# The stores of the attention rows, begun by ScalarE on its own DMA queue instead of by SyncE

## The reference

```python
proj = einsum('btd,de->bte', x, w_in) + b_in          # q, k, v, conv value, conv gate
q, k = rope(q, pos), rope(k, pos)
attn = banded_window_attention(q, k, v, sinks)        # 8 heads of 64, 2 kv heads, window 128
u    = ca * sigmoid(cg)
conv = silu(layer_norm(depthwise_causal_conv(u)))     # width 31, 512 channels
mix  = concat([attn, conv]) @ w_out + b_out
h    = layer_norm(ALPHA * x + mix)
f    = hier_moe(h)                                    # top-1 group of 4, top-2 of its 8 experts
y    = layer_norm(ALPHA * h + f)
```

## Time and profile before

| | before |
|---|---|
| median of 3 runs | 1359.54 us |
| profiled execution, its own time | 1357.34 us |
| span of its trace | 1355.5 us |
| busy: PE, DVE, ACT, POOL | 1251.7, 737.0, 537.2, 471.5 us |
| busy shares | 92%, 54%, 40%, 35% |
| mean granted TensorE clock | 0.971 |
| DMA queue of SP (q1): share of the 16 engines' span | 47.2% |
| DMA queue of ACT (q10) | 0.8% |

### The profile page before, as it was taken

The page is one execution under the profiler, slowest core; times in us unless marked ns, Lnnn a source line. Parts: engine busy times, 40 slices in busy tenths (PEclk is TensorE's granted clock), DMA queues, the critical chain, the costliest instruction groups (busy, mean ns, idle before and its releaser), DMA issues.

```text
span 1355.5 us, 21260 instructions
## 1 busy us (share of the span) xinstructions
PE 1251.7 (92%) x5579; PEld 600.6 (44%) x5580; DVE 737.0 (54%) x2093; ACT 537.2 (40%) x883; POOL 471.5 (35%) x633
## 2 busy tenths in 40 slices
PE   8999998999999998799999999899999999999910
PEld 3444445666666665345555545333333333333300
DVE  2434334565465555468888887544444444444348
ACT  0000001344344433423333332366666656666544
POOL 5113210000000000345555554355666666665321
PEclk9999999999999998899999999999999999999965
DMA  6375645231221174256666544289899999999686
GB/s 260 95 220 161 182 150 164 79 112 60 78 71 48 63 234 147 98 201 219 220 220 190 153 143 140 76 260 336 273 325 366 328 290 344 318 367 354 192 273 261
DMA packets 91256, 273.41 MB, mean 202 GB/s; under 512 B 14888, under 2 KB 41088, under 8 KB 78038
## 3 DMA queue, kind: packets, MB, share of 16 engines
q1 hardware_dynamic: 73975, 226.53, 47.2%
q0 software_dynamic: 14384, 42.32, 13.0%
q10 hardware_dynamic: 2807, 3.53, 0.8%
HBM read 212.80 MB, written 66.40 MB: 206 GB/s over the span
## 4 chain that ended last, share of the span: by engine, by line
PE 46%; issue 30%; DVE 11%; DVEq 6%; DMA 3%; ACT 2%; POOL 1%; POOLq 1%; ACTq 1%; SPq 1%
PE P L1130 13%; PE bank_S L1152 9%; PE M L1130 6%; PE bank_S L744 4%; PE P L744 3%; DVEq L1723 3%; PE bank_T L744 2%; PE M L744 2%; DVE route L1728 2%; PE M L1138 1%; DVE work L1685 1%; PE bank_S L918 1%; DMA work<-conv_rows 1%; DMA big<-sum_rows 1%; ACT work L1447 1%
## 5 line engine op out<-in xcount | busy, mean ns | idle before, releaser
L1397 ACT ACTIVATE big<-big 128x2048 f32 x76 | 145.0, 1910 | 121.1 <-issue 71.8
L1130 PE MATMUL P<-big,work 128*64 x416 | 188.0, 595 | 1.7 <-DVE work L1943 1.5
L1131 PE MATMUL P<-big,work 128*64 128x512 f32 x416 | 188.0, 595 | 0.0
L783 PE MATMUL P<-big,work 128*128 128x256 f32 (+1 forms) x512 | 172.6, 493 | 3.7 <-DMA work<-in_xt_prompt 3.7
L2134 POOL DMA_INDIRECT work<-h_rows,piece_idx x148 | 141.9, 959 | 63.2 <-issue 40.4
L1152 PE MATMUL bank_S<-big,work 128*64 x304 | 136.7, 592 | 1.0 <-DVE work L1927 1.0
L1154 PE MATMUL bank_S<-big,work 128*64 128x512 f32 x304 | 136.7, 592 | 0.0
L2050 POOL TENSOR_SCALAR work<-work 128x1 f32<-128x1 f32 (+1 forms) x17 | 3.8, 221 | 364.4 <-DVE work L1606 364.3
L783 PEld LDWEIGHTS P<-big,work 128*128 128x128 f32 x512 | 96.0, 191 | 74.3 <-issue 64.3
L918 PE MATMUL P<-big,work 128*128 128x512 f32 x256 | 115.9, 606 | 6.2 <-DMA work<-attn_cols 6.2
L918 PE MATMUL bank_S<-big,work 128*128 128x512 f32 x256 | 113.8, 598 | 0.0
(11 more groups left out here) (356 smaller groups left out, 2262.9 us busy)
## 6 DMA issues: line engine op xcount, KB each, us to landing
big<-in_w SPq DMA_DIRECT2D x96, 1024.0 KB, 10.9
work<-in_xt_prompt SPq DMA_DIRECT2D x32, 512.0 KB, 4.3
big<-sum_rows SPq DMA_DIRECT2D x16, 520.0 KB, 8.2
big<-in_toe SPq DMA_DIRECT2D x16, 512.0 KB, 3.3
work<-in_x_prompt SPq DMA_DIRECT2D x16, 512.0 KB, 3.9
h_rows<-work SPq DMA_DIRECT2D x16, 512.0 KB, 2.7
sum_rows<-work SPq DMA_DIRECT2D x16, 512.0 KB, 3.6
out_y_prompt<-big SPq DMA_DIRECT2D x16, 512.0 KB
```

Source lines behind the costliest of these rows:

```text
L783: last = mm(dst[0:n, 0:c1 - c0], lhs[:, k, :], w_qkv[:, k, c0:c1], start=(k == 0), stop=(k == KD - 1))
L1130: mm(lower, xgT[j][:, k, 0:U], both[:, k], start=(k == 0), stop=(k == KD - 1))
L1131: last = mm(upper, xgT[j][:, k, U:P], w_up[:, k], start=(k == 0), stop=(k == KD - 1))
L1397: fn(w_up.rearrange("p k m f -> p m k f")[:, :, ks, :], src, ACT.Copy).then_inc(s[f"wu{part}_ok"], 1)
```

## The change

SP's wait for `at_ev` and its begin of the store go. ACT waits for the count of its own copy and begins the same store, right behind the copy and ahead of whatever follows on ACT in that step. The semaphores, the buffer, the sizes and the order of all else are as before.

```diff
@@ SyncE, in the loop over steps
-                if 0 <= t - 1:
-                    after(sp, s["at_ev"], t - 1)
-                    sp.dma_start(at_dram[t - 1], at_sb).then_inc(s["at_st"], 16)
@@ ScalarE, in the loop over steps
                     after(act, s["pe_vB"], t - 1)
                     after(act, s["at_st"], t - 2, per=16)
                     fn(at_sb, M0[:, :], ACT.Copy).then_inc(s["at_ev"], 1)
+                    after(act, s["at_ev"], t - 1)
+                    act.dma_start(at_dram[t - 1], at_sb).then_inc(s["at_st"], 16)
```

## The result

| | before | changed |
|---|---|---|
| median of the paired runs | 1358.56 us, 4 runs (1356.84 to 1360.55) | 1343.97 us, 4 runs (1343.34 to 1346.29) |
| ratio | | 0.9895, 95% interval 0.9876 to 0.9915 |
| profiled execution, its own time | 1357.34 us | 1346.29 us |
| span of its trace | 1355.5 us | 1344.4 us |

The change makes the kernel 14.6 us faster by the medians. The profiled execution of the changed kernel is the slowest of its four runs, and against the profiled one of before it gains 11.05 us. A second measurement beside other runs of before gave 1344.65 against 1358.27 us, 13.6 less, ratio 0.9897 (0.9882 to 0.9912).

A forecast was written before the change was run, and what follows sets the result against it. PE, busy 92% of the span, was taken as the bound, so only its idle or low-clock stretches count. Terms -6.6 - 8.4 + 0 = -15.0 gave 1342.3, or 1344.6 with the median's 2.2; forecast 1344, range 1340.5 to 1353.5.

The forecast's parts named there:

- the second chain: Step 17: SP's late store delays bias and attention rows, so PE waits 6.21 us; removing this forecast at 8.4 us.
- (a): Steps 14 and 15: ACT begins tile 11's store at about 488.4, landing by 497; worth 6.6 us.
- (b): Step 17: bias and attention rows begun some 10 us or more earlier, PE's wait goes whole; worth 8.4 us.
- what is late next?: Within (b): the bias chain, DVE's L1642, ends by 561 and PE wants it at 566; five us of slack.
- (c): ACT's price for 16 begins at about 0.45 us, mostly in gaps; taken as 0, upper bound 1.5 us.
- (d): Steps 15 to 17: SP runs ahead, expert matrices begun back to back; cost 0, bounded by 1 us.
- (e): Price of ACT's begin while SP is stuck in one of 10.94 us; taken as 0.5 to 1.1 us, covered.
- rivals 1 and 2: ACT's begin held to SP's backlog end, 1364 (0.09; as no change 0.10), or for 10.94 us only, 1352 (0.10).
- Rival 3: Second chain returns only its wait; bias chain or first tile's normalization takes its place: 1353, chance 0.08.
- Rival 4: Store's data crawl behind SP's 7 MB, land after 508, step 15's copy still waits: 1351 at worst, chance 0.03.

## Why the prediction was right, and where it was not

The time was forecast as 1344 and came to 1343.97 us. Most of the mechanism is right, but that closeness is partly luck. The sum was made against the profiled execution and gave 1342.3; the two profiled executions of the changed kernel took 1346.29 and 1344.65. Two terms were off, with opposite signs: the second chain was taken 4.0 to 4.5 us too large, and a third gain of 1.8 us was put at nothing. The 2.2 us by which the median of before stood above its profiled execution (1.2 with the fourth run) were added, and the median of after stands 2.3 below the first of its two.

**(a) Steps 14 and 15: right.** Forecast 6.6, measured 6.61, and 7.1 by the medians where it stands alone. Its reasoning "lands by 497" was wrong: the pace of a store behind the backlog on SP was carried over to a store beside it. It landed at 505.2, and the copy is free from 505.84. The gain was right by 0.6 us, not by the 7.7 that the prediction believed it had.

**(b) Step 17: the mechanism right, the size wrong.** This is the step that failed: forecast 8.4, measured 3.9 and 4.4 in the two profiles of the changed kernel. The wait for the rows went whole, as said, and the 16 records behind it took 7.24 us, near the 7.03 of full clock. The failure is in "what is late next?". That question was put only to what comes behind the bias (L1642, five us of slack, and it kept them). It was not asked what the early bias sets free to run: POOL's two operations, which had stood beside nothing critical, now stand beside DVE's L1540, on which the last flips wait. The wait of PE grew from 1.2 to 3.6 us, and the lower clock behind it nearly doubled the two flips and `values` (1.97 us each for 1.09). With POOL held back the term measures 8.37, so the sum of waits was right and the collision, 4.3 us from turn to projection (17.64 against 13.31 of before), was the missing term. Of the prediction's own signs, "the clock stays full from 480 to 600" failed (0.68 from 550 to 560), and the new idle stretch lies just ahead of its "between 550 and 600", from 546.34 to 549.98.

The last sentence of (b), that the steps after gain slack too, was right and was given no value; the stretch up to the routing is 1.85 and 1.77 us shorter.

**(c) and (d): right.** The kernel in which only the begins move gains its 6.6 and loses nothing that shows. ACT's begin of 0.33 us was even below the 0.45 taken, and SP's running ahead delayed no x tile.

**(e) and rivals 1 and 2: they fall.** Their common premise was that ACT's begin is held while SP is stuck in one. 0.33 us inside 4.77 says no, as the earlier trace rows had, and the one at 489.23 took 0.33 us as well. That the begins do share something shows only with four in a row. The rule of the Trainium skill on exclusive use ("Perfetto Trace Analysis", section "DMA Instruction — HWDGE (DVE, Sync)") is not borne out by these rows for a single begin, if SP held that block through its whole 4.77 us.

**Rival 3: half true.** "Another wait takes its place" is what happened, with 4.3 us of the 8.4, but neither of the two waits that it named. It was given 0.08 and the argument of the five us against it answered only its first name.

**Rival 4: nearly true.** It was given 0.03 with "16 us of time for 256 KB" against it. The store took 16.0 us. 256 KB are 128 packets of 2 KB; one for one with packets of 33 KB these need 128 x 33 KB = 4.2 MB of SP's data to pass, by estimate 10.7 us at the 396 GB/s measured, besides what else stood there. The argument of the prediction counted the bytes of the store and not its turns. The copy did not wait only because 0.6 us were left.

## What to carry to other kernels

When a wait is removed from an in-order queue, list everything behind it and ask of each item not only who waits for it but what it starts, and which engine that work will run beside; and give each freed item a value, even where it is only "more slack". A gain that rests on a transfer landing in time needs the size of the packets beside it, not only the number of bytes ahead. And the total of a queue's waits says little: of SP's 103.6 us, those of the ordinary steps, in which PE was never idle, were worth nothing, while 20 us of stuck begins ahead of one small store were worth 6.6.

## What the runs showed of the hardware

- A DVE operation of 128x4 elements (L1540, both inputs in SBUF) took 2.24 us in place of 0.16 and ended with POOL's 128x1024 addition (548.14 and 548.12). So it was in five kernels of this study (2.24, 2.25, 2.24, 2.25, and 2.07 where it started 0.29 us into the addition), and never where POOL was idle. The Trainium skill has the mechanism ("SBUF — State Buffer", section "SBUF: two separate sides"): DVE and GpSimd share a pair of ports that one of them holds for a whole instruction. For the addition the length agrees.
- For POOL's scaling of 2.79 us it does not. The first L1540 took 0.71, 0.43, 0.53, 0.46 and 0.96 us in five profiles, and in each ended 1.05 or 1.06 us after the scaling had started; in the kernel with the weights twice it started 1.06 us after it and took its 0.16. L1542, also of 128x4, started 1.12 us after it (543.97 for 542.85) and took 0.16. So DVE was held for the first 1.05 us of the scaling at most and not for the rest. Why is open.
- A begin on ACT took 0.33 us with SP stuck in one of 4.77 us, but up to 1.74 us where four followed each other.
- Two queues with work share the DMA engines in turns that do not go by bytes: 80 packets of 33 KB to 71 of 2 KB, but 1679 of 0.5 KB to 142 of 2 KB. A 256 KB store took 16.0 and 15.1 us beside the 4 MB load (two profiles of the changed kernel), 16.7 with 8 MB, 6.5 beside the smaller packets, 2.0 in the median.
